# Two inner norms by token stream, with latents ahead of context, and half the products of constants

## The reference, cut to what matters

```python
def rms_norm(x, g):
    xf = x.astype(jnp.float32)
    y = xf * lax.rsqrt(jnp.mean(xf * xf, axis=-1, keepdims=True) + EPS)
    return (y * g.astype(jnp.float32)).astype(x.dtype)
...
        x = x + g1 * o
        x = x + g2 * swiglu(modulate(rms_norm(x, norm2_g[l]), sh2, sc2), ffn_w_in[l], ffn_w_out[l])
        if need_ctx:
            cx = cx + cg1 * oc
            cx = cx + cg2 * swiglu(modulate(rms_norm(cx, norm2_g[l]), csh2, csc2), ffn_w_in[l], ffn_w_out[l])
```

## Time and profile before

| | us |
|---|---|
| three runs | 1183.45, 1183.32, 1185.31 |
| median | 1183.45 |
| the profiled execution: its own time | 1183.81 |
| its span in the trace | 1182.0 |
| PE busy | 1153.1 |
| DVE busy | 764.9 |
| ACT busy | 486.0 |

### The profile page before, as it was taken

The page is one execution under the profiler, slowest core; times in us unless marked ns, Lnnn a source line. Parts: engine busy times, 40 slices in busy tenths (PEclk is TensorE's granted clock), DMA queues, the critical chain, the costliest instruction groups (busy, mean ns, idle before and its releaser), DMA issues.

```text
span 1182.0 us, 17884 instructions
## 1 busy us (share of the span) xinstructions
PE 1153.1 (98%) x7354; PEld 937.4 (79%) x7354; DVE 764.9 (65%) x1235; ACT 486.0 (41%) x745; POOL 11.2 (1%) x19
## 2 busy tenths in 40 slices
PE   8999999999999999999999989999999999999998
PEld 5777777777688888888888777899565898998997
DVE  5599979753665546656546368987779546554455
ACT  4423337553442322222222333466368636443442
POOL 2000000000000000000000000000000000000000
PEclk9999999999999999999999989999999999999999
DMA  9855460023665556775545323334000153555551
GB/s 349 315 169 170 156 219 2 29 88 123 234 213 167 183 176 203 243 235 166 167 151 196 111 65 113 108 112 160 15 1 1 55 178 113 192 178 182 193 167 64
DMA packets 124659, 176.21 MB, mean 149 GB/s; under 512 B 5437, under 2 KB 103335, under 8 KB 123431
## 3 DMA queue, kind: packets, MB, share of 16 engines
q1 hardware_dynamic: 124150, 174.62, 45.3%
q10 hardware_dynamic: 433, 0.51, 0.2%
HBM read 172.76 MB, written 1.05 MB: 147 GB/s over the span
## 4 chain that ended last, share of the span: by engine, by line
PE 87%; DVE 8%; ACT 3%; issue 1%; ACTq 0%; DVEq 0%
PE acc L2230 20%; PE acc L2232 20%; PE acc L2231 20%; PE acc L2314 2%; PE acc L2315 1%; PE acc L2316 1%; PE p L2607 1%; PE p L2608 1%; PE p L2609 1%; PE pmod L2508 1%; PE p L2062 1%; DVE sm L1562 1%; PE p L2477 1%; PE p L2067 1%; DVE Y L1480 1%
## 5 line engine op out<-in xcount | busy, mean ns | idle before, releaser
L666 ACT ACTIVATE w_hi<-raw 128x1024 fp32r<-128x1024 f32 (+1 forms) x224 | 212.8, 998 | 408.9 <-PE acc L2232 361.4
L676 DVE TENSOR_TENSOR w_lo<-raw,w_hi 128x1024 fp32r<-128x1024 f32 x222 | 244.6, 1144 | 190.9 <-ACT w_hi L666 190.7
L2230 PE MATMUL acc<-Hhi,w_hi 128*128 128x512 f32 (+1 forms) x960 | 327.1, 341 | 1.4 <-DVE w_lo L676 1.4
L2232 PE MATMUL acc<-Hhi,w_lo 128*128 128x512 f32 (+1 forms) x960 | 324.4, 338 | 0.0
L2231 PE MATMUL acc<-Hlo,w_hi 128*128 128x512 f32 (+1 forms) x960 | 324.3, 338 | 0.0
L2230 PEld LDWEIGHTS acc<-Hhi,w_hi 128*128 128x128 f32 x960 | 182.1, 190 | 27.4 <-issue 6.2
L2232 PEld LDWEIGHTS acc<-Hhi,w_lo 128*128 128x128 f32 x960 | 182.1, 190 | 19.7
L2231 PEld LDWEIGHTS acc<-Hlo,w_hi 128*128 128x128 f32 x960 | 182.2, 190 | 18.9
L2230 PE MATMUL acc<-hid_hi,w_hi 128*128 128x512 f32 x248 | 98.0, 395 | 1.2 <-DVE w_lo L676 1.2
L2231 PE MATMUL acc<-hid_lo,w_hi 128*128 128x512 f32 x248 | 96.6, 390 | 0.0
L2232 PE MATMUL acc<-hid_hi,w_lo 128*128 128x512 f32 x248 | 96.6, 390 | 0.0
(11 more groups left out here) (398 smaller groups left out, 1640.1 us busy)
## 6 DMA issues: line engine op xcount, KB each, us to landing
raw<-in_ffn_w_in SPq DMA_DIRECT2D x44, 1024.0 KB, 5.4
piece<-in_mod_w SPq DMA_DIRECT2D x64, 512.0 KB, 5.0
raw<-in_mod_w SPq DMA_DIRECT2D x18, 1024.0 KB, 5.4
raw<-in_od_w_in SPq DMA_DIRECT2D x15, 1024.0 KB, 5.3
raw<-in_ffn_w_out SPq DMA_DIRECT2D x12, 768.0 KB, 7.3
raw<-in_ev_w_in SPq DMA_DIRECT2D x8, 1024.0 KB, 7.5
raw<-in_od_w_out SPq DMA_DIRECT2D x8, 1024.0 KB, 4.9
raw<-in_ffn_w_out SPq DMA_DIRECT2D x8, 1024.0 KB, 5.0
```

Of the source, the lines that this page charges most:

```text
L666: nc.scalar.activation(w_hi[:, w % 2, c0:c1], raw[:, r % RAW_SLOTS, c0:c1], ACT.Copy)\
L676: nc.vector.tensor_tensor(w_lo[:, w % 2, c0:c1], raw[:, r % RAW_SLOTS, c0:c1], w_hi[:, w % 2, c0:c1].bitcast(F32), ALU.subtract).then_inc( ...
L2230: mm(outs[m], hi[:, j, cols], xh, start=(first and j == 0), stop=False)
L2232: ins = mm(outs[m], lo[:, j, cols], xh, start=False, stop=(last and j == kts - 1))
```

## The change

Norms 1 and 2 go over the latents and then over the context. Block q = 6 is made in halves of 256 columns. Block q = 7 is made for the latents and then for the context, and counts `first_done` as it goes. While its context half runs, DVE, ACT and PE update, square and sum the latents' tiles. Root, reciprocal, spreading, `gained`, high and `low` are made for one stream and then for the other; context updates and the split of the pair's second weight block (its high part on ACT and its low part on DVE) stand between them. The pair is made by `paired_streams`: all of both blocks for the latents, then all for the context, in products of 256 columns; either block counts as done in the context's second half. Norm 1's modulation products 5 and 6 move between the first tiles of the pair. In norm 2 the squares and sums of tiles 4 and 5 move from block 7 to block 6. Layer 0's last output pair of the mixer uses bank 1, so block 0 of the pair needn't wait for the context's update. The counts of products of constants go from 6, 9, 6 and 6 to 3, 4, 3 and 3.

```diff
+                step(A(sm[:, 0, 7:8], epsc[:, 0:1], ACT.Sqrt))
+                square_stream(n, 6, 0, updates)
+                square_stream(n, 7, 0, updates)
+                stream_root(0)
+                for f in range(4):
+                    high(f, 0)
+                square_stream(n, 6, 1, updates)
+                split(block, parts=(0,))
+                square_stream(n, 7, 1, updates)
+                split(block, parts=(1,))
+                for f in range(4, 7):
+                    high(f, 0)
+                stream_root(1)
+                high(7, 0)
+                for f in range(KD):
+                    high(f, 1)
...
-                    for f in SUMS_AT[n == 1].get(q, ()):
+                    for f in SUMS_AT[n < 3].get(q, ()):
...
+                if n < 3:
+                    return
...
+                updated(0, 0)
+                updated(1, 0)
+                stream_inverse(0)
+                dve.wait_ge(s("rs_spread"), 2 * n)
+                gained(0, 0)
+                for f in range(3):
+                    gained(f + 1, 0)
+                    low(f, 0)
+                updated(0, 1)
+                low(3, 0)
+                updated(1, 1)
+                gained(4, 0)
+                split(block, parts=(0,))
+                for f in range(4, 7):
+                    gained(f + 1, 0)
+                    low(f, 0)
+                stream_inverse(1)
+                low(7, 0)
+                split(block, parts=(1,))
+                dve.wait_ge(s("rs_spread"), 2 * n + 1)
+                gained(0, 1)
+                for f in range(KD):
+                    if f + 1 < KD:
+                        gained(f + 1, 1)
+                    low(f, 1)
...
+            def sum_stream(n, f, v):
+
+                pe.wait_ge(s("sq_ready"), SQ_BASE[n] + 2 * v + f + 1)
+                for g in (2 * v, 2 * v + 1):
+                    ins = mm(p5[32 * g:32 * g + 32, v * P:v * P + P], cst("ones", 0, 32),
+                             n_sq[:, f % 2, g * P:(g + 1) * P], start=False, stop=(f == KD - 1))
+                ins.then_inc(s("ss_mm"), 1)
...
+            def paired_streams(n, blocks, enter, units=()):
+
+                between = {(0, 1): units[0:1], (0, 2): units[1:2]}
+                for v in range(2):
+                    cols = slice(v * LAT, (v + 1) * LAT)
+                    for j0 in (0, KD // 2):
+                        for b, (outs, hi, lo, width) in enumerate(blocks):
+                            if v == 0:
+                                enter(b, j0)
+                            for j in range(j0, j0 + KD // 2):
+                                if v == 0:
+                                    for k in between.get((b, j), ()):
+                                        mod_unit(2 * KD + k)
+                                    if (b, j) == (0, 3):
+                                        sum_stream(n, 6, 1)
+                                    if (b, j) == (1, 2):
+                                        sum_stream(n, 7, 1)
+                                    if (b, j) == (0, 7):
+                                        spread_stream(n, 1)
+                                pe.wait_ge(s("h_lo"), H_BASE[n] + KD * v + j + 1)
+                                xh, xl = Hhi[:, j, cols], Hlo[:, j, cols]
+                                for m, o in enumerate(outs):
+                                    wide = slice(m * width, (m + 1) * width)
+                                    mm(o[:, cols], hi[:, j, wide], xh, start=(j == 0), stop=False)
+                                    mm(o[:, cols], hi[:, j, wide], xl, start=False, stop=False, skip_group_check=True)
+                                    ins = mm(o[:, cols], lo[:, j, wide], xh, start=False, stop=(j == KD - 1))
+                            if v and j0:
+                                ins.then_inc(block_done, 1)
+
+            def product_streams(n, outs, hi, lo, rhs, kts, upper):
+
+                for v in range(2):
+                    cols = slice(v * LAT, (v + 1) * LAT)
+                    for m, o in enumerate(outs):
+                        for j in range(kts):
+                            if v == m == 0 and j == 4:
+                                upper()
+                            if v and m * kts + j == 0:
+                                sum_stream(n, 6, 0)
+                            if v and m * kts + j == 5:
+                                sum_stream(n, 7, 0)
+                            wide = slice(m * P, (m + 1) * P)
+                            xh, xl = (x[:, cols] for x in rhs(j))
+                            mm(o[:, cols], hi[:, j, wide], xh, start=False, stop=False, skip_group_check=True)
+                            mm(o[:, cols], hi[:, j, wide], xl, start=False, stop=False, skip_group_check=True)
+                            ins = mm(o[:, cols], lo[:, j, wide], xh, start=False, stop=(j == kts - 1), skip_group_check=True)
+                        ins.then_inc(block_done if v and m else s("first_done"), 1)
+                spread_stream(n, 0)
...
-                for f in SUMS_AT[n == 1].get(q, ()):
-                    sum_square(n, f, t)
-                if q == 7:
-                    fill = GATE_UNITS[0] if n == 1 else ()
-                    for k in fill[:1]:
-                        mod_unit(2 * KD + k)
-                    if n == 3:
-                        keep_clock(6)
+                for f in SUMS_AT[n < 3].get(q, ()):
+                    if n == 3 or f < 6:
+                        sum_square(n, f, t)
+                if q == 7 and n == 3:
+                    keep_clock(3)
                     spread_roots(n, t)
-                    for k in fill[1:]:
-                        mod_unit(2 * KD + k)
-                    if n == 3:
-                        keep_clock(6)
-
...
+                        if last is not None:
+                            pe.wait_ge(read_dve, last)
...
+                            part_ready(w, 0)
+                            paired_streams(1, pair_, second_weights(1, w, R["dve"]), GATE_UNITS[0][1:])
...
+                        if half == 1 and q == 6:
+                            product_halves([acc[:, 2 + m, :] for m in range(2)], w_h, w_l,
...
+                        if half == 1 and q == 7:
+                            product_streams(2, [acc[:, 2 + m, :] for m in range(2)], w_h, w_l,
...
-            pe.wait_ge(read_dve, FFN_READS[0][3]["dve"] + 4)
+            pe.wait_ge(read_dve, FFN_READS[0][3]["dve"] + 3)
...
-            keep_clock(6)
+            keep_clock(3)
...
-            keep_clock(9)
+            keep_clock(4)
...
-BANK_OF = ((0, 1, 2, 0), (0, 1, 0, 1))
+BANK_OF = ((0, 1, 2, 1), (0, 1, 0, 1))
...
-FIRST_AGAIN = ({6: 1}, {4: 1, 6: 2})
+FIRST_AGAIN = ({6: 2}, {4: 1, 6: 2})
```

More of the change, by code:

```diff
@@ L664, in split @@
                         eng.wait_ge(block_done, at(w - 1, it, 4))
-                    for c0, c1 in ((0, low), (low, n)):
+                    for part in parts:
+                        c0, c1 = ((0, low), (low, n))[part]
                         nc.scalar.activation(w_hi[:, w % 2, c0:c1], raw[:, r % RAW_SLOTS, c0:c1], ACT.Copy)\
@@ L1037, in _ @@
             ffn(0, T)
-            norm(2, T, C_IN + 1)
+            norm_streams(2, FFN_READS[0][3]["dve"], C_IN + 1)
             w = C_IN
@@ L1758, in ffn @@
                                 mod_half(9)
-                            if q == 7:
-                                dve.wait_ge(s("first_done"), 2)
-                                update(l, G2, 1, 6, t, norm=2)
-                            elif q % 2:
+                            if q % 2 and q < 7:
                                 dve.wait_ge(block_done, w + q + 1)
@@ L1835, in conv_pair @@
                             step(ins)
-            norm(2, T, C_IN + 1)
+            norm_streams(2, G2, 1, C_IN + 1)
             w = C_IN
@@ L2549, in out_block @@
                 b = BANK_OF[l][pair]
+                if l == 0 and n == 6:
+                    product_halves([acc[:, 2 * b + m, :] for m in range(2)], w_h, w_l,
+                                   lambda j: (hi[:, kt * part + j, :], lo[:, kt * part + j, :]), kt,
+                                   lambda: part_ready(w + n, 1))
+                    square_sums(1, 6, T)
+                    return
+                if l == 0 and n == 7:
+                    product_streams(1, [acc[:, 2 * b + m, :] for m in range(2)], w_h, w_l,
+                                    lambda j: (hi[:, kt * part + j, :], lo[:, kt * part + j, :]), kt,
+                                    lambda: part_ready(w + n, 1))
+                    square_sums(1, 7, T)
+                    return
                 product([acc[:, 2 * b + m, 0:t] if b < 2 else p67[:, m, 0:t] for m in range(2)], w_h, w_l,
@@ L2681, in ffn_out @@
                                 kt, first=(q % 2 == 0), last=(q % 2 == 1),
-                                apart=half == 1 and q == 7,
```

136 lines of the change are left out of this document (108 added, 28 removed).

## The result

| | before | changed |
|---|---|---|
| median of 15 runs each (us) | 1184.08 | 1186.66 |
| lowest, highest | 1183.20, 1185.31 | 1186.13, 1187.47 |
| the profiled execution's own time | 1183.81 | 1187.46 |
| its span | 1182.0 | 1185.7 |

The ratio is 1.0022, with a 95% interval of 1.0014 to 1.0029: the change makes the kernel slower by 2.6 us. The forecast was 1183.0, the same time, and the measured one stands at the very end of its range. Part of the distance of 3.7 us is not the change's: the median before was 1183.45 over three runs and is 1184.08 over fifteen. The forecast was a change of -0.4 us, the measured one is +2.6, so 3.0 us have to be explained. The profiled execution of the changed kernel is one of its slowest, 0.8 us above the median, and the experiments will say why.

A forecast was written before the change was run, and what follows sets the result against it. PE, busy 1153.1 of 1182.0 us, was taken as the bound: its products' cost and its waits. +1.7 + 1.4 - 2.0 - 1.5 = -0.4 against 1183.81 gave 1183.4, as a median 1183.0 us; range 1178.6 to 1186.7.

The forecast's parts named there:

- norm 1 up to the pair's end: Norm 1's pair: 3.2 us of waits go, 3.6 of halves, interruptions and pieces come; +0.4 us.
- its seam, wait for `f_gate`: Behind norm 1's pair: block 0 ends later, so the next gate block waits 1.3 to 1.5 us for ACT; 1.3 taken.
- norm 2 up to the pair's end: Norm 2's pair: -2.0 of waits, -2.3 of slow clock, +3.3 of halves, interruptions and pieces; -1.0 us.
- its seam, wait for `w_lo`: Block behind the dt block: DVE's chain starts later, so PE's wait grows from 1.4 to 3.9 us.
- attention's constants: Layer 1's attention, around sums and scores: fewer counts of constants let PE arrive earlier; -2.0 us.
- norm 3's constants: Norm 3: fewer constants let spreading and pair start earlier, less 0.4 to 0.5 of a wait; -1.5 us.
- norm 2's clock: Norm 2's pair: no remaining wait as long as 2.91 us, so the clock stays full and 2.3 us come back.
- products cut in two: Norm 1: 168 products cut into halves, each costing 0.0133 us more; +2.2 us.
- ways in and out of interruptions: Norm 1: six further interruptions of PE's products at 0.2 us each; +1.2 us.
- The 1.1 us wait at the second block: Norm 2's pair: PE waits 1.1 us for DVE's low weights before the second block.
- The one whose constants only covered waits: Scores and norm 3: DVE and ACT set the pace, so the 2.0 and 1.5 don't come; 1186.5 us, chance 0.08.
- The rival of the falling clock: Scores and norm 3: with halved constants PE idles and drops to 1.2 GHz; +4.6, 1187.6 us, chance 0.10.

The follow-up runs named there:

- second profile: The changed kernel, unaltered, run once more for another profile: 1186.55 us.
- the block by block version: Changed kernel with all of block 0 before all of block 1 in the context's half of either pair: 1180.56 us, ratio 0.9970.
- the constants alone: Kernel before with the counts of products of constants halved (3, 4, 3, 3) and no streams: 1179.85 us, ratio 0.9966.
- no counts: Kernel before with 3 and 5 counts of constants added in norm 2 and none at the old four places: 1182.21 us.
- the best version with streams: Changed kernel with the context's half of either pair block by block and block q = 6 in whole 512-column products: 1179.67 us.
- the one without: Kernel before, no streams, counts of constants halved and 3 and 5 counts added in norm 2: 1178.38 us, ratio 0.9947.
- 1 count: Kernel before with 3 and 5 counts of constants added in norm 2 and 1 at each of the old four places: 1179.96 us.

## Why the prediction was wrong

**Step by step.**

| term | predicted | in the two traces |
|---|---|---|
| norm 1 up to the pair's end | +0.4 | +1.5 |
| its seam, wait for `f_gate` | +1.3 | +1.6 (wait 1.34) |
| norm 2 up to the pair's end | -1.0 | -1.0 |
| its seam, wait for `w_lo` | +2.5 (wait 3.9) | +2.6 (wait 3.97) |
| the block behind that wait | 0 | +2.8 (+1.6 in the second profile) |
| attention's constants | -2.0 | -2.4 |
| norm 3's constants | -1.5 | -1.4 |
| sum | -0.4 | +3.7 |

The sum of the predicted rows is -0.3; the prediction took a tenth off norm 2 for pieces of the copy, which makes +1.4 and -0.4.

**The step that failed is norm 2's clock.** The prediction took the fall of the earlier trace rows out, with the reason that no wait left in norm 2 is as long as the 2.91 us behind which it fell. The next paragraph computed a wait of 3.9 us at the seam, longer than that one, and never asked what the clock does behind it. The price was in hand, 2.3 us; with it the sum would have been +1.9 and the forecast 1185.3. It was an omission, not an unknown: constants in that wait bring 1.7 us back in the medians, and in the block by block version, where the wait is 1.09, the block runs at full clock.

The reason itself was too weak as well. "1.27 and 1.48 led to none" was read from one trace, and other traces show a fall behind each of them: behind 1.48 with the constants alone, behind 1.27 and 0.61 with no counts. In norm 2's pair the clock falls behind 1.72 or 1.73 us in four of six profiles. That the term of -2.3 came out in the profiled execution was partly luck; it cost little when it didn't, 0.3 us net, because the wait of 0.86 us went with it. And the 2.3 us of slow products were not all to be had: with constants in norm 2 the first eleven spacings take 2.75 us (684.37 to 687.12) and not 2.49, and 1.8 us is left at `p<-stack,dtT` (724.70 against 722.93).

**The second step is the size of norm 1's pair**, 1.1 us of it. Taken apart from 280.64 (280.65 in the changed kernel) to the pair's end, by distances between starts:

| part | predicted | in the two traces |
|---|---|---|
| waits of PE (2.93 before, 0.73 after) | -2.3 | -2.2 |
| products cut in two (168) | +2.2 | +2.1 |
| ways in and out of interruptions, less DVE's pace inside the pair | +0.3 (1.2 - 0.9) | +0.6 |
| sums, spreading and units in pieces | +0.2 | +1.0 |

The last row is the mis-sized one. The sums take 1.95 us in place of 1.24, the spreading 1.27 in place of 1.08: a sum over half a tile's columns takes 0.34 us (307.05 to 307.39), while two whole tiles' sums took 0.57 together before.

**What held.** Both seams, their mechanism, releasers and sizes (1.34 against 1.3 to 1.5, 3.97 against 3.9), shown by the block by block version, which undoes both. The price of a cut, as far as the runs resolve it. The full clock in norm 2's pair in the profiled execution, though not in each. The 1.1 us wait at the second block: 0.86. All that the prediction named as a sign of being wrong stayed away (PE met both waits, the spacing is 0.12, the clock holds behind 874 and 984), and it was wrong all the same: the list had no entry for the clock behind the seam. The gain of the constants, 3.8 in the traces against 3.5, 4.2 alone. DVE's wait of 1.41 for scores is gone, and norm 3's pair starts 2.0 us earlier against its sum of squares (988.91 - 982.31 before, 992.02 - 987.42 now), as computed:

```profile
885.43 1.22 DVE L2112 TENSOR_REDUCE smC<-acc 128x2 f32<-128x1024 f32 x1
...
992.02 0.36 PE L2502 MATMUL acc<-Hhi,w_hi 128*128 128x256 f32 x1 [0.29 <-DVE Hlo L1514]
```

**The rivals.** None of them happened as told. The one whose constants only covered waits comes within 0.2 us of the result (1186.5 against 1186.66), by luck: the constants alone give 4.2 us, and the loss lies elsewhere. The rival of the falling clock had the right mechanism, idleness and then half the clock, at the wrong places: it looked at the halved constants, where the clock held, and not at the seam, where the longest wait of all was. The Trainium skill's rule there (TensorE: Matmul & The Clock Gate, section What's actually happening), that the slow clock is the default and activity releases it, agrees with all of these traces: each slow stretch stands behind idleness, and constants in its place, which compute nothing, keep 2.4 GHz.

**What stays open.** Behind the same wait a fall costs 1.6 us in one execution and 2.8 in another, and behind waits of 1.72 us it comes in some and not in others. What decides when it comes wasn't settled; only that the dearer execution is the one whose slow stretch was twice as long. The streams were not tried in norm 2 alone; from the landmarks of the best version with streams (724.62 behind norm 2's seam, of which 1.3 belongs to norm 1) against the one without (722.93) they would about tie, an estimate that no run tested.

## What to carry to other kernels

Whoever reorders work to shorten a wait should list each wait that the order makes longer and price it twice: its own length, and the engine's clock behind it, by the dearest fall that the trace shows. A wait isn't safe because it is shorter than the one that was punished in a single trace: here falls stand behind 1.48 and 1.72 us too. When two blocks are interleaved, what matters to those behind is when the first one ends, so the interleaving should last only as long as it feeds the engine: here finishing block 0 first in the context's half was worth 6.1 us. And where a wait can't be had shorter, products of constants in it may give more than the reordering: eight counts in norm 2 gave 2.1 us with no instruction moved.

## What the runs showed of the hardware

- The clock's fall is not a fixed price. In the profiles it took 1.8 us in norm 2 of the kernel before (724.70 against 722.93 with constants in norm 2), and 1.2 in the version with the constants halved, where it fell at 681.2, during the spreading, and rose at 688.1. Behind waits of 3.97 to 3.98 it took 2.8, 1.6 and 1.6. The medians give 2.1 for the first place and 1.7 for the last. One profile gives the size of such a term only within a factor of two.
- What an execution pays is about half of the time in which PE works at 1.2 GHz. In the changed kernel's first profile that is 6.0 us (718.39 to 724.4) for 2.8, in its second 3.4 us (719.3 to 722.7) for 1.6. In norm 2 of the kernel before, 1.8 us of the slow stretch (682.6 to 689.4) passed while PE waited anyway.
- A single wait of 1.72 or 1.73 us, in norm 2 or at the scores, had no fall behind it in three profiles and one in four. In norm 3 a fall began 0.1 us into such a wait, behind one of 1.44. Falls stand also behind waits of 0.61 and 1.48 (norm 2, constants halved) and of 1.27 and 0.61 (norm 1, no counts), where other profiles with the same waits have none.
- The granted clock of each run shows falls without a profile: in the seven runs with 1 count it goes from 0.999 to 0.996 as the time goes from 1178.14 to 1181.36 us. The spread of the times alone says less: it is 0.4 us over five runs with waits filled, 3.2 over seven and 4.6 over eleven with fewer or no counts, but also only 0.5 over five in the version with the constants halved, where norm 2's waits aren't filled.
- Each interruption of a row of products in these norms costs PE about 0.2 us besides its own work, 0.1 ahead of it (306.84 to 307.05 in place of 0.12) and 0.1 at the second product behind it (307.39 to 307.62).
